# Two transformer blocks on one core: the output projections as three products of rounded operands

## The reference

```
first block (1 layer):  x = x + gt1 * (concat(a, g) @ w_out)      # 512 x 1024 @ 1024 x 1024
                        x = rms_norm(x + gt2 * moe(...))
second block (2 layers): y = g0*(y_na@na_w_o) + g1*(y_gm@gm_w_o) + g2*(y_mla@mla_w_o)
                         mix = y @ w_out[i]                        # 1024 x 1024 weights
                         x_new = x + gt1 * mix, then a feed-forward part
                         ctx is updated in the same way unless the layer is the last
```

## Time and profile before

| what | value |
|---|---|
| median of 3 runs | 4066.74 us (4065.21 to 4068.7) |
| the profiled execution | 4065.76 us, its span 4063.9 us |
| TensorE busy | 3450.8 us, 85% of the span |
| DVE, ACT, POOL busy | 1472.7, 1047.0, 585.2 us |
| granted TensorE clock, mean | 0.926 of full speed |

### The profile page before, as it was taken

The page is one execution under the profiler, slowest core; times in us unless marked ns, Lnnn a source line. Parts: engine busy times, 40 slices in busy tenths (PEclk is TensorE's granted clock), DMA queues, the critical chain, the costliest instruction groups (busy, mean ns, idle before and its releaser), DMA issues.

```text
span 4063.9 us, 40443 instructions
## 1 busy us (share of the span) xinstructions
PE 3450.8 (85%) x15843; PEld 2311.0 (57%) x15843; DVE 1472.7 (36%) x2594; ACT 1047.0 (26%) x1853; POOL 585.2 (14%) x459
## 2 busy tenths in 40 slices
PE   5996764787782999788999799999599898998998
PEld 2664543232332875445665488888485455646886
DVE  3226542000004446551212433333474551115444
ACT  3112411211112225442111222221234442103221
POOL 1000001000003325122110100000344122201000
PEclk8998786999996999899999899999799899998999
DMA  7883022899996310002112211111621003123222
GB/s 264 331 313 116 1 104 64 340 427 429 428 394 197 86 45 10 8 34 91 36 58 83 93 63 63 63 63 52 183 69 33 9 34 122 62 104 116 92 95 81
DMA packets 159781, 533.96 MB, mean 131 GB/s; under 512 B 9532, under 2 KB 64724, under 8 KB 136572
## 3 DMA queue, kind: packets, MB, share of 16 engines
q1 hardware_dynamic: 136252, 401.04, 26.6%
q0 software_dynamic: 16880, 92.26, 6.5%
q10 hardware_dynamic: 6480, 38.34, 2.4%
HBM read 488.84 MB, written 42.78 MB: 131 GB/s over the span
## 4 chain that ended last, share of the span: by engine, by line
PE 59%; DVE 4%; ACT 2%; DVEq 1%; DMA 1%; issue 1%; POOL 1%; ACTq 0%; POOLq 0%
PE ps L2748 11%; PE ps L2754 11%; PE ps L1838 6%; PE ps L1840 6%; PE ps L1839 6%; PE ps L2523 5%; PE ps L509 4%; PE ps L2051 4%; PE ps L2103 2%; PE ps L2091 2%; PE ps L2085 1%; DVE Z L2651 1%; DVEq L219 1%; DMA ring<-in_w_out_dram 1%; DVE small L2191 0%
## 5 line engine op out<-in xcount | busy, mean ns | idle before, releaser
L2748 PE MATMUL ps<-hT_hi,w_hi 128*128 128x512 f32 (+1 forms) x768 | 275.3, 359 | 28.1 <-DVE w_lo L2802 28.1
L2748 PE MATMUL ps<-hT_hi,w_lo 128*128 128x512 f32 (+1 forms) x768 | 276.0, 359 | 0.0
L2748 PE MATMUL ps<-hT_lo,w_hi 128*128 128x512 f32 (+1 forms) x768 | 275.8, 359 | 0.0
L1838 PE MATMUL ps<-wp_hi,hT_hi 128*128 128x512 f32 (+2 forms) x608 | 222.1, 365 | 38.1 <-POOL wp_lo L1817 38.1
L2754 PE MATMUL ps<-w_hi,h_hi 128*128 128x512 f32 x640 | 253.7, 396 | 0.0
L2754 PE MATMUL ps<-w_hi,h_lo 128*128 128x512 f32 x640 | 253.7, 396 | 0.0
L2754 PE MATMUL ps<-w_lo,h_hi 128*128 128x512 f32 x640 | 253.6, 396 | 0.0
L1838 PE MATMUL ps<-wm_hi,hT_hi 128*128 128x512 f32 x480 | 215.0, 448 | 28.4 <-POOL wm_lo L2493 28.4
L2051 PE MATMUL ps<-Z 64*128 64x256 f32 (+3 forms) x576 | 201.6, 548 | 28.5 <-DVE small L2193 11.6
L1840 PE MATMUL ps<-wp_hi,hm_lo 128*128 128x512 f32 (+2 forms) x608 | 220.4, 363 | 0.0
L1839 PE MATMUL ps<-wp_lo,hT_hi 128*128 128x512 f32 (+2 forms) x608 | 220.3, 362 | 0.0
(11 more groups left out here) (437 smaller groups left out, 6154.1 us busy)
## 6 DMA issues: line engine op xcount, KB each, us to landing
pj<-in_expert_w_up_dram SPq DMA_DIRECT2D x32, 2048.0 KB, 18.1
pj<-in_expert_w_down_dram SPq DMA_DIRECT2D x32, 2048.0 KB, 19.7
ring<-in_expert_w_gate_dram SPq DMA_DIRECT2D x32, 2048.0 KB, 16.0
ring<-in_ffn_w_dram SPq DMA_DIRECT2D x64, 1024.0 KB, 5.3
ring<-in_w_in_dram SPq DMA_DIRECT2D x58, 1024.0 KB, 6.6
Z<-in_w_mod_dram POOLq DMA_DIRECT2D x24, 2048.0 KB, 8.0
Z<-in_w_ada_dram POOLq DMA_DIRECT2D x8, 2048.0 KB, 9.2
ring<-in_w_out_dram SPq DMA_DIRECT2D x6, 2048.0 KB, 16.3
```

The costliest lines, as they stand in the source:

```text
L1838: nc.tensor.matmul(out_, a_hi, b_hi, start=first, stop=False)
L2748: last = nc.tensor.matmul(bank(i % 8, c1 - c0), W[a][:, k, :], r[:, k, c0:c1], start=(k == 0 and r is hhk and a == 0), stop=(k == KT - 1 a ...
```

## The change

The turn stages now write the input in two parts: ACT copies each unit, rounded, into `hT_hi`, and DVE subtracts that from the same bank into `al_lo`. So both engines handle every unit. The weights come in four pieces of 1 MB (x = 0 to 3: column block x // 2, half x % 2 of the input width), in three slots of the ring. Each piece is split by ACT (`act_out`, into `w1_hi` for even x, another place for odd x) and by DVE (`dve_out`, in place in its slot of the ring). The first piece is split at the end of the turn stage. TensorE (`pe_out`) then runs over the pieces: for each piece all tiles, 4 x 3 matmuls each. Piece 3 goes into slot 0, so its transfer waits until TensorE has finished piece 0 (`wo_half`).

```diff
+        def act_turn3(act, n, nt, q):
+            p = plan_turn3(n, nt)
+            for i in range(2 * nt):
+                t, h = i // 2, i % 2
+                act.wait_ge(mm_done, p.done(i))
+                act.activation(hhk[:, 4 * h:4 * h + 4, P * t:P * t + P], bank(i % 8).rearrange("p (k n) -> p k n", k=4), ACT.Copy).then_inc(turn_hi, 1)
+            act_out(act, q, 0)
+
+        def dve_turn3(dve, n, nt, q):
+            p = plan_turn3(n, nt)
+            for i in range(2 * nt):
+                t, h = i // 2, i % 2
+                dve.wait_ge(turn_hi, p.g0 + i + 1)
+                nc.vector.tensor_tensor(al(nt)[:, 4 * h:4 * h + 4, P * t:P * t + P], bank(i % 8).rearrange("p (k n) -> p k n", k=4),
+                                        hhk[:, 4 * h:4 * h + 4, P * t:P * t + P], ALU.subtract).then_inc(evac_v, 1)
+            dve_out(dve, q, 0)
+
+        def out_hi(q, x):
+
+            if x % 2 == 0:
+                return w1_hi[:, :].rearrange("p (k n) -> p k n", n=512)
+            return zo_hi[:, :].rearrange("p (k n) -> p k n", n=512) if q == 0 else pj_r[:, :].rearrange("p (t n) -> p t n", t=TA)[:, 0:4, NQ:NQ + 512]
+
+        def out_lo(x):
+            return w1_lo[:, 2048 * (x % 3):2048 * (x % 3) + 2048].rearrange("p (k n) -> p k n", n=512)
+
+        def out_used(p, nt, q, x):
+
+            return (wo_half, 2 * q + x // 2 + 1) if x % 2 == 0 else (mm_done, p.done(nt * (x // 2 + 1) - 1))
+
+        def sp_out(sp, n, rel, w, blocks, q):
+            p, nt = plan_lin(n, blocks), len(blocks[0][2])
+            for r in rel:
+                if r:
+                    sp.wait_ge(mm_done, r)
+            for x in range(4):
+                if x == 3:
+                    sp.wait_ge(*out_used(p, nt, q, 0))
+                nb, kh = x // 2, x % 2
+                sp.dma_start(W1[x % 3].rearrange("p (k n) -> p k n", n=512),
+                             w[512 * kh:512 * kh + 512, 512 * nb:512 * nb + 512].rearrange("(k p) n -> p k n", p=P)).then_inc(wo_in[x % 3], 16)
+            rel[0] = rel[1] = p.done(2 * nt - 1)
+
+        def act_out(act, q, x, p=None, nt=None):
+            act.wait_ge(wo_in[x % 3], 32 * q + 16 * (x // 3 + 1) if x % 3 == 0 else 16 * q + 16)
+            if x >= 2:
+                act.wait_ge(*out_used(p, nt, q, x - 2))
+            act.activation(out_hi(q, x), W1[x % 3].rearrange("p (k n) -> p k n", n=512), ACT.Copy).then_inc(wo_hi_ok, 1)
+
+        def dve_out(dve, q, x):
+            dve.wait_ge(wo_hi_ok, 4 * q + x + 1)
+            nc.vector.tensor_tensor(out_lo(x), W1[x % 3].rearrange("p (k n) -> p k n", n=512), out_hi(q, x), ALU.subtract).then_inc(wo_lo_ok, 1)
+
+        def pe_out(pe, n, blocks, q):
+            p, nt = plan_lin(n, blocks), len(blocks[0][2])
+            for x in range(4):
+                nb, kh = x // 2, x % 2
+                pe.wait_ge(wo_lo_ok, 4 * q + x + 1)
+                for t in blocks[0][2]:
+                    i = nt * nb + t
+                    if kh == 0 and i >= 8:
+                        pe.wait_ge(evac_v, p.val[i - 8])
+                    for k in range(4):
+                        kk = 4 * kh + k
+                        last = three(bank(i % 8), hhk[:, kk, P * t:P * t + P], al(nt)[:, kk, P * t:P * t + P],
+                                     out_hi(q, x)[:, k, :], out_lo(x)[:, k, :], kk == 0, kk == KT - 1)
+                    if kh:
+                        last.then_inc(mm_done, 1)
+                    elif t == nt - 1:
+                        last.then_inc(wo_half, 1)
+
+        def act_outs(act, n, blocks, q):
+            p, nt = plan_lin(n, blocks), len(blocks[0][2])
+            for x in (1, 2, 3):
+                act_out(act, q, x, p, nt)
+
+        def dve_resid(dve, n, blocks, q):
+            p, nt = plan_lin(n, blocks), len(blocks[0][2])
             tmp = [Z[:, 7168:7680], Z[:, 7680:8192]]
             n["gate"] = n.get("gate", 0) + 32
             dve.wait_ge(gate_in, n["gate"])
-            for c0, c1, ts, *_ in blocks:
+            dve_out(dve, q, 1)
+            for nb, (c0, c1, ts, *_) in enumerate(blocks):
+                dve_out(dve, q, 2 + nb)
                 for t in ts:
+                    i = nt * nb + t
                     dve.wait_ge(mm_done, p.done(i))
                     nc.vector.tensor_tensor(tmp[i % 2], bank(i % 8), gtb[:, t // TL, c0:c1], ALU.mult).then_inc(evac_v, 1)
                     dve.drain()
                     nc.vector.tensor_tensor(xl[:, t, c0:c1], xl[:, t, c0:c1], tmp[i % 2], ALU.add)
...
-            plan_t(n, acc_pairs(l))
-            sp_lin(sp, n, rel, I["w_out_2"][l], WO2(l))
+            plan_turn3(n, len(TQ[l]))
+            sp_out(sp, n, rel, I["w_out_2"][l], WO2(l), 1 + l)
             sp.wait_ge(stage_done, f0 + 4 * 8)
             sp.dma_start(xl[:, :, :].rearrange("p t d -> p (t d)"), xspill).then_inc(x_back, 16)
```

More of the change, by code:

```diff
@@ L168, in program @@
         ybuf = nc.dram_tensor("ybuf", (NBLK * CAP, D), F32, kind="Internal").ap()
+        al_lo, zo_hi, pj_r = over("al_lo", "Z", 0, 6144), over("zo_hi", "Z", 4096, 2048), over("pj_r", "pj", 0, TA * PW)
         stage_done = sem("stage_done")
+        wo_in, wo_hi_ok, wo_lo_ok, wo_half, turn_hi = [sem(f"wo_slot{i}_in") for i in range(3)], sem("wo_hi_ok"), sem("wo_lo_ok"), sem("wo_half"), sem("turn_hi")
         w1_in, w1_hi_ok, w1_lo_ok, w1_half = [sem(f"w1_slot{i}_in") for i in range(3)], sem("w1_hi_ok"), sem("w1_lo_ok"), sem("w1_half")
@@ L1353, in load_gate, with plan_turn3, al, pe_turn3 @@
                 eng.dma_start(gtb[:, w, :], modd[l, w, D * s:D * s + D].partition_broadcast(P)).then_inc(gate_in, 16)
-        def dve_resid(dve, n, blocks):
-            p = plan_lin(n, blocks)
-            i = 0
+        def plan_turn3(n, nt):
+            p = Plan(n, "v" * (2 * nt))
+            p.g0 = n.get("t3", 0)
+            n["t3"] = p.g0 + 2 * nt
+            return p
+        def al(nt):
+            return al_lo[:, 0:KT * P * nt].rearrange("p (k n) -> p k n", k=KT)
+        def pe_turn3(pe, n, nt, src):
+            p = plan_turn3(n, nt)
+            for i in range(2 * nt):
+                t, h = i // 2, i % 2
+                if i >= 8:
+                    pe.wait_ge(evac_v, p.val[i - 8])
+                for k in range(4):
+                    last = nc.tensor.transpose(bank(i % 8)[:, P * k:P * k + P], src(4 * h + k, t), ident)
+                last.then_inc(mm_done, 1)
@@ L2838, in WO2 @@
             return [(0, 512, TQ[l], "v"), (512, 1024, TQ[l], "v")]
-        def acc_pairs(l):
-            return [(acc[:, t, P * k:P * k + P], hTk[:, k, P * t:P * t + P]) for t in TQ[l] for k in range(KT)]
         STAGES2 = 12
@@ L3006, in _ @@
                 plan(n)
-            plan_turn(n, KT, LAT)
-            sp_lin(sp, n, rel, I["w_out"][0], WO1)
+            plan_turn3(n, TL)
+            sp_out(sp, n, rel, I["w_out"][0], WO1, 0)
             sp.wait_ge(stage_done, 4 * 10)
@@ L3147, in _ @@
             load_gate(act, 0, 2)
-            each_turn(act, n, "a", KT, LAT, hT_dst)
+            act_turn3(act, n, TL, 0)
             fence(act, n)
-            plan_lin(n, WO1)
+            act_outs(act, n, WO1, 0)
             fence(act, n)
```

23 lines of the change are left out of this document (11 added, 12 removed).

## The result

| | median | lowest to highest | executions |
|---|---|---|---|
| before | 4067.11 us | 4062.37 to 4070.94 | 12 |
| changed | 4074.97 us | 4069.68 to 4081.28 | 12 |

The ratio is 1.0022, its 95% interval 1.0013 to 1.0031: slower by 0.22%, in us by 5.3 to 12.6. The forecast was 4075 us, with a chance of 0.48 for slower.

What follows compares the result with a forecast made beforehand. TensorE, busy 85% of the span, was taken to bound each projection through its matmuls. Terms -4.1, +5.5 and +7.0 gave +8.4 us on the profiled 4065.76, so 4074.2, about 4075 us in the runs; range 4063 to 4088.

Steps and rivals of the forecast that it cites:

- sum of the three terms: Output projections: first block -4.1 us, second block's layer 0 +5.5 and layer 1 +7.0, together +8.4 us.
- The mechanism and its place: Layers 0 and 1: after piece 0 TensorE stands 15.6 us until the `xl` reload lands and DVE splits piece 1.
- The rival with a reload of 22.9 us: Layers 0 and 1: the `xl` reload takes as long as before, 10 us more per layer, 4095 us; chance 0.12.
- The product's distance: Output projections: rounded products 0.234 us apart, three replacing a float32 matmul of 0.863 us; gain 35 us at full clock.
- That rival: Output projections: a rounded product costs 0.216 us, 12 us less, 4063 us, no measurable change; chance 0.04.
- The slow clock: TensorE after gaps: 2.0 us lost in the first block, 2.4 at each later layer's start, 1.5 after each stall.
- The rival that the clock stays up: TensorE keeps full clock over the gaps: up to 9.8 us less, 4065 us; counted within the likeliest case's spread.
- The turn stages: Before each projection: ACT and DVE work delays TensorE's start to 580.15, 2205.1 and 3600.3, from 575.92, 2202.07 and 3599.90.
- Layer 1's term: Second block's layer 1 projection: products end at 3664.7 against 3657.7, +7.0 us, including a 15.6 us stall.
- At no cost: Later expert loads (some 17 us), feed-forward weights issued at the out stage's end, and bank releases stay hidden.
- a stage outside the touched ones which moves by more than 2 us: Sign against the prediction: any stage outside the six touched ones moving by more than 2 us makes it wrong.
- The rival in which the stall doesn't form: Layers 0 and 1: reload is in SBUF when piece 0 ends, kernel faster at 4041 us; chance 0.06.

Runs made afterwards that it cites:

- two experiments: Against the changed kernel: SP issues the `xl` reload ahead of the `wo_half` wait, 4038.54 us; or DVE waits for it only behind splits of pieces 1 and 2, 4040.95 us.
- five kernels: Changed kernel with reload issued earlier, 4038.54 us; DVE's wait later, 4040.95; both, 4041.16; both plus first block's early first split, 4040.26, or its loads ahead of `wo_half`, 4041.53.

## Why the prediction was right

The times of the forecast were given in the frame of the profile before. The changed kernel reaches the first transpose 0.67 us earlier than that, layer 0's `w_out` issue 1.70 us earlier (2191.53 and 2189.83) and layer 1's 4.16 us later (3588.87 and 3593.03). With these offsets taken out, its rows stand against the forecast like this:

| | forecast | measured |
|---|---|---|
| first block: start, end of products | 580.15, 627.1 | 579.99, 627.01 |
| layer 0: start, stall, restart, end | 2205.1, 15.6, 2239.9, 2291.9 | 2204.33, 14.71, 2238.62, 2291.36 |
| layer 1: start, stall, restart, end | 3600.3, 15.6, 3629.5, 3664.7 | 3599.61, 14.88, 3627.70, 3662.76 |
| sum of the three terms | -4.1 +5.5 +7.0 = +8.4 | -4.15 +4.9 +5.1 = +5.9 |

- *The mechanism and its place were right*: the waits, the chain and two experiments, each of which takes one of its two halves away, show it. The stall was 0.7 to 0.9 us too long in the forecast. The reload needed 11.8 and 12.0 us, where I had 12.6 and 0.6 for issue and signals, taken from a reload that followed a larger chunk. The rival with a reload of 22.9 us is out.
- *The product's distance was right*, 0.2333 us for pieces that use `w1_hi` and 0.230 for those in `pj_r`, against 0.234. The Trainium skill (TensorE: Matmul & The Clock Gate, "Wait — 56ns, not 53.3ns?") gives 215.7 ns at full clock for 512 columns and 426.7 ns at half of it. At 1.2 GHz the products here agree with the second figure, 0.427 us. At 2.4 GHz they don't agree with the first: they are 14 to 18 ns longer. That rival is out.
- *The slow clock cost what was forecast in sum, but not in its parts.* A product at 1.2 GHz costs 0.427 - 0.233 = 0.194 us more (I had 0.448 for 0.427). The first block was slow for 4.0 us (1.8 us lost, forecast 2.0), layer 0's start for 5.4 (2.5, forecast 2.4), layer 1's for 3.9 (1.8, forecast 2.4), the restarts for 5.3 and 3.1 us (2.4 and 1.4, forecast 1.5 each). 9.9 us against 9.8. The rival that the clock stays up is out: the granted clock is 0.50 behind each gap. And without the stall layer 0 becomes 17.7 us shorter and layer 1 16.5, which is the stall and 3.0 and 1.6 us more, of which the slow clock is 2.4 and 1.4.
- *The turn stages* were right within 0.2 us in the first block and 0.8 and 0.7 us too long in the two layers: DVE's unit takes 0.605 us in layer 0, not 0.66, and ACT's 0.50 in layer 1 (8 in 4.03 us), not 0.56.
- *Layer 1's term was mis-sized most*, +7.0 against +5.1: 0.7 us at the start, 0.4 in piece 0, 0.7 in the stall. The three profiles of before also differ by 1.3 us in this stretch.
- *At no cost* was right for the feed-forward part: TensorE's wait for its first split is 15.4 us, as before 15.98. For the first block it was not: the stretch behind it, up to the experts' loop, is 1.6 us longer. The one part seen in every profile, 0.33 us, is DVE's pause and not the loads; for the rest the loads are neither shown nor excluded as the cause.
- *The whole is further up than the stages*: the three stages give +5.9 us, and with the 1.6 us lost behind the first block, of which I had nothing, it is +7.5; the medians give +7.9, with 5.3 to 12.6 by the interval. So a part of the agreement of 4075 with 4074.97 is luck: my stages were 2.5 us too dear, and the program lost some of the first block's gain behind it. That the change is slower was a close call as well: my sum lay on my own border of 0.2%, with 0.48 for slower against 0.43 for the same, and with 1 us less the measured 0.22% would be on its other side.
- *Where I said that a stage outside the touched ones which moves by more than 2 us would make me wrong*, this sign appeared. The first pair of profiles shows two such stages, +2.4 us in layer 0's attention and -2.8 us in layer 1's (246.62 and 243.81, from the load of `mla_w_ukv`). The bound was too tight: three profiles of the kernel before differ by 4.3 us in layer 0's, taken from the same load, and by 1.6 in layer 1's (245.07 to 246.62), where the nine others lie at 243.6 to 246.0.

The rival in which the stall doesn't form was priced at 4041 us. It doesn't come by itself, SP's list holds the reload as I had read it, but as an edit it came out at 4038.5 to 4041.5 in five kernels. It is the version to keep, either edit alone: 0.7% below the kernel before, where the change as it stands is 0.2% above. Without the stall the three stages are 28 us shorter than before (4.1, 12.7 and 11.3 us by the means of the table): the 35 us of the products less the longer starts and the slow clock. The two stalls with their slow clock had taken 34 us of it back.

## What to carry to other kernels

A wait in an engine's list holds everything behind it, so when new work is put into a list, look at each wait that now stands ahead of it, and ask who waits for the new work. The old wait for `xl` was 17 us long and free, because only residuals stood behind it; with a weight split behind it, it cost 15 us of TensorE in each layer. The same holds for a queue of transfers: a piece that waits for a buffer takes with it every transfer behind it, however early that one could go. Move the transfer with no such condition ahead, or the wait down to its first real user; one of the two is enough.

## What the runs showed of the hardware

- After gaps of nearly the same length, 14.71 and 14.88 us, TensorE ran at 1.2 GHz for 5.3 us in layer 0 and for 3.1 us in layer 1. After gaps of 5.0, 5.75 and 5.46 us it was 4.0, 5.4 and 3.9 us. The length of the gap doesn't set the length of the slow stretch here.
- The same rounded product is 0.2333 us apart from the next with weights in one buffer and 0.230 in another. I don't know why.
- DVE pauses for 0.42 us at one point of the routing part, with no wait that the profile shows. In the three profiles of before it does so where nobody waits for it, in the nine with a changed first block a few operations earlier, on TensorE's path; 35.97 us became 36.30 us there, though the instructions weren't edited. The cause is open; the loads beside it aren't it.
